# Stick-breaking tails as two rounded passes, 400-column row groups and no engine barriers in a two-block transformer kernel

## The reference, cut to what matters

```
z = (q @ k.T) * scale
log_beta = log_sigmoid(z)
log_keep = where(past, log_sigmoid(-z), 0)
tail = reverse_cumsum(log_keep) - log_keep      # sum over the later keys
a = where(past, exp(log_beta + tail), 0)
out = a @ v
```

## Time and profile before

| | before |
|---|---|
| time, median of 3 runs | 1644.75 us (1641.38 to 1645.51) |
| profiled execution, own time | 1644.14 us |
| its span, first to last instruction | 1642.3 us |
| TensorE busy | 1589.6 us, 97% |
| VectorE, ScalarE, GpSimd busy | 888.2, 669.4, 120.6 us |
| mean granted TensorE clock | 0.996 of full speed |

### The profile page before, as it was taken

One profiled execution on the slowest core, in us unless ns is written; L12 is line 12 of the kernel. 1 busy time (PEld: TensorE's weight loads), 2 busy tenths in 40 slices (PEclk: granted clock), 3 DMA queues, 4 the chain that ended last, 5 costly groups with the idle time before them and its releaser, 6 DMA issues.

```text
span 1642.3 us, 27109 instructions
## 1 busy us (share of the span) xinstructions
PE 1589.6 (97%) x11727; PEld 1285.9 (78%) x11727; DVE 888.2 (54%) x1386; ACT 669.4 (41%) x1005; POOL 120.6 (7%) x138
## 2 busy tenths in 40 slices
PE   7999999998999999999999999999899999999998
PEld 5856778776895798888888898777568888888887
DVE  5455586442634364555454654436875766555644
ACT  4316843324334264334141254656883532221210
POOL 1310106000000010000000020012300000000000
PEclk9999999999999999999999999999999999999999
DMA  7611223320630335536453533321003243333322
GB/s 241 185 52 52 76 89 100 113 85 30 198 132 23 128 123 187 183 105 228 128 179 128 179 87 109 77 77 52 2 27 103 62 118 85 96 103 103 94 78 86
DMA packets 154073, 176.66 MB, mean 108 GB/s; under 512 B 14600, under 2 KB 111506, under 8 KB 153570
## 3 DMA queue, kind: packets, MB, share of 16 engines
q1 hardware_dynamic: 145004, 162.24, 31.0%
q10 hardware_dynamic: 8950, 12.69, 2.6%
HBM read 168.31 MB, written 8.43 MB: 108 GB/s over the span
## 4 chain that ended last, share of the span: by engine, by line
PE 85%; DVE 7%; ACT 5%; issue 2%; DMA 1%; ACTq 0%; SPq 0%; DVEq 0%; POOL 0%
PE ps L397 63%; PE ps L848 4%; PE ps L1471 4%; PE ps L824 1%; PE ps L2066 1%; PE ps L3135 1%; DMA sb_arena<-sb_arena 1%; DVE weights_low L420 1%; PE ps L2892 1%; ACT weights_high L417 1%; PE ps L2880 1%; PE ps L2912 1%; PE ps L1049 1%; PE ps L765 1%; DVE sb_hT L2988 1%
## 5 line engine op out<-in xcount | busy, mean ns | idle before, releaser
L420 DVE TENSOR_TENSOR weights_low<-sb_weights_raw,weights_high 128x2048 fp32r<-128x2048 f32 (+2 forms) x117 | 263.9, 2255 | 260.2 <-ACT weights_high L417 260.0
L397 PE MATMUL ps<-left_high,weights_high 128*128 128x512 f32 (+1 forms) x888 | 352.0, 396 | 2.3 <-DVE left_low L718 2.1
L397 PE MATMUL ps<-left_low,weights_high 128*128 128x512 f32 (+1 forms) x888 | 345.9, 390 | 0.0
L397 PE MATMUL ps<-left_high,weights_low 128*128 128x512 f32 (+1 forms) x888 | 345.9, 390 | 0.0
L417 ACT CAST weights_high<-sb_weights_raw 128x2048 fp32r<-128x2048 f32 (+2 forms) x117 | 219.4, 1875 | 299.3 <-PE ps L397 261.6
L397 PEld LDWEIGHTS ps<-left_high,weights_high 128*128 128x128 f32 (+1 forms) x888 | 166.0, 187 | 47.5 <-issue 9.2
L397 PEld LDWEIGHTS ps<-left_high,weights_low 128*128 128x128 f32 (+1 forms) x888 | 166.0, 187 | 36.0
L397 PEld LDWEIGHTS ps<-left_low,weights_high 128*128 128x128 f32 (+1 forms) x888 | 166.1, 187 | 35.5 <-issue 1.7
L397 PE MATMUL ps<-weights_high,hidden_high 128*128 128x512 f32 x432 | 169.1, 391 | 0.0
L397 PE MATMUL ps<-weights_high,hidden_low 128*128 128x512 f32 x432 | 168.2, 389 | 0.0
L397 PE MATMUL ps<-weights_low,hidden_high 128*128 128x512 f32 x432 | 168.1, 389 | 0.0
(11 more groups left out here) (445 smaller groups left out, 2463.1 us busy)
## 6 DMA issues: line engine op xcount, KB each, us to landing
sb_weights_raw<-in_w_in SPq DMA_DIRECT2D x25, 1024.0 KB, 5.2
sb_yT<-in_ada_w SPq DMA_DIRECT2D x24, 1024.0 KB, 5.3
sb_weights_raw<-in_ffn_w_up SPq DMA_DIRECT2D x44, 512.0 KB, 4.8
sb_weights_raw<-in_mlp_w_up SPq DMA_DIRECT2D x16, 1024.0 KB, 5.8
sb_weights_raw<-in_mlp_w_down SPq DMA_DIRECT2D x16, 1024.0 KB, 7.5
sb_weights_raw<-in_ffn_w_down SPq DMA_DIRECT2D x10, 1024.0 KB, 5.1
sb_weights_raw<-in_xattn_w_kv SPq DMA_DIRECT2D x8, 1024.0 KB, 5.3
sb_weights_raw<-in_w_out SPq DMA_DIRECT2D x6, 1024.0 KB, 5.1
```

Source lines behind the costliest of these rows:

```text
L397: last = nc.tensor.matmul(o, lhsT, rhs, start=b["first"] and i == 0, stop=b["last"] and i == len(pairs) - 1)
L420: nc.vector.tensor_tensor(l[:, 0:n], raw[:, 0:n], h[:, 0:n].bitcast(F32), ALU.subtract).then_inc(w_low, 1)
```

## The change

- Barriers: `stage_end` and its four uses are gone. In their places stand waits for what is needed: the grams wait per PSUM bank for the inversion's reads, the recurrence waits for all kept grams, TensorE waits for all eight banks of the query projection before cross attention. The grams' first dense step (after the third gram) is left out there and so comes at the grams' end.
- Rows: the 256-column and the 144-column row chunks become one of 400 columns, loaded as two chunks of 4 k-tiles each (upper, lower), four pieces each. As two token tiles fit the two banks, the order is: upper for tiles 0 and 1, lower for them, upper again for tiles 2 and 3, lower again for them ("again" chunks are neither loaded nor split a second time). A step is now 12 multiplications of 400 columns.
- Tails: ScalarE rounds the softplus into EX_HIGH (`high`), VectorE subtracts it in place to get the remainder (`low`), ones and triangle are rounded once into ONES_TRI by VectorE, and TensorE multiplies each block twice, by the high and by the low part.
- Order: the numbers of dense steps between the parts change as shown. SP loads the second half of the bias tables after the chunk 0 to 256 instead of after 1024 to 1280, and waits for all four heads' tails before.

```diff
+        ROWS_AT, ROWS_W = 512, 400
+        def stick_and_sparse_rows():
+            columns = (2052, 2308), (2756, 2820), (2884, 2960), (1536, 1540)
+            def blocks(half, tiles):
+                return [by_token(0, ROWS_W, h_rows(t), "dve", dve_copy_to(VB[:, t, ROWS_AT:ROWS_AT + ROWS_W]), nk=4,
+                                 k0=4 * half, first=half == 0, last=half == 1) for t in tiles]
+            upper, lower = (chunk_of([W2K[:, 4 * half:4 * half + 4, x:y] for x, y in columns], blocks(half, (0, 1)))
+                            for half in range(2))
+            return [upper, lower] + [dict(pieces=[], again=ch, nk=4, width=ROWS_W, blocks=blocks(half, (2, 3)))
+                                     for half, ch in enumerate((upper, lower))]
...
-            chunk_of(w2((2052, 2308)), trow(0, 256, 512)),
+            *stick_and_sparse_rows(),
...
-            chunk_of(w2((2756, 2820), (2884, 2960), (1536, 1540)), trow(0, 144, 768)),
...
         def front_pe(pe):
...
-            fill(dense, 4)
+            fill(dense, 2)
...
             def tails(pair, e):
-                pe.wait_ge(st_sp, 2 * pair + e + 1)
+                pe.wait_ge(split_low, pe.count(split_low))
                 for kt in range(NT):
                     for k2 in range(kt, NT):
                         o = AT_KT[kt] + (k2 - kt) * P
-                        last = nc.tensor.matmul(st_sums(e)[:, o:o + W_KT[k2]], cst("tri") if k2 == kt else ones,
-                                                st_part(EX[e], k2), start=k2 == kt, stop=k2 == NT - 1)
+                        for low, part in enumerate((EX_HIGH[:, e, :], EX_LOW[e])):
+                            last = nc.tensor.matmul(st_sums(e)[:, o:o + W_KT[k2]], ONES_TRI[:, int(k2 == kt), :],
+                                                    st_part(part, k2), start=k2 == kt and not low,
+                                                    stop=k2 == NT - 1 and low == 1)
...
             scores(0)
-            fill(dense, 4)
+            fill(dense, 6)
             tails(0, 0)
...
             scores(1)
-            fill(dense, 4)
+            fill(dense, 6)
             tails(1, 0)
             fill(dense, 1)
             tails(1, 1)
-            fill(dense, 2)
+            fill(dense, 1)
             times_v(1)
...
+            def high(pair, e):
+                a.wait_ge(st_sp, 2 * pair + e + 1)
+                nc.scalar.copy(EX_HIGH[:, e, :], EX[e]).then_inc(split_high, 1)
...
             logs(0)
             nc.scalar.preload_act_table_set(EXP_SET)
             fill(dense, 4)
+            high(0, 0)
+            high(0, 1)
+            fill(dense, 2)
             weights(0, 0)
...
             logs(1)
             nc.scalar.preload_act_table_set(EXP_SET)
-            fill(dense, 4)
-            split_weights(a, "act", w_in_2[6]["index"])
+            fill(dense, 2)
+            high(1, 0)
+            high(1, 1)
+            fill(dense, 2)
+            split_weights(a, "act", w_in_2[8]["index"])
             weights(1, 0)
...
+            def low(e):
+                v.wait_ge(split_high, v.count(split_high))
+                nc.vector.tensor_tensor(EX_LOW[e], EX[e], EX_HIGH[:, e, :].bitcast(F32),
+                                        ALU.subtract).then_inc(split_low, 1)
...
+            nc.vector.tensor_copy(ONES_TRI[:, :, :].rearrange("p a b -> p (a b)"),
+                                  consts[:, cst_at["ones"][0]:cst_at["ones"][0] + 2 * P])
             scaled(0, 0)
             scaled(0, 1)
-            fill(dense, 2)
+            fill(dense, 4)
             softplus(0, 0)
             softplus(0, 1)
+            low(0)
+            low(1)
             fill(dense, 2)
             exponents(0, 0)
...
             fill(dense, 1)
             softplus(1, 0)
             softplus(1, 1)
+            low(0)
+            low(1)
             fill(dense, 3)
+            split_weights(v, "dve", w_in_2[8]["index"])
             exponents(1, 0)
-            split_weights(v, "dve", w_in_2[6]["index"])
...
-            stream_weights(sp, STREAM[w_in_2[4]["index"]:w_in_2[7]["index"]])
+            stream_weights(sp, STREAM[w_in_2[7]["index"]:w_in_2[11]["index"]])
+            sp.wait_ge(st_tail, 4)
             load_bias_sp(sp, range(4, 8))
...
             invert_pe(pe, memory)
-            pe.stage_end()
             grams_pe(pe, memory)
-            pe.stage_end()
             scan_pe(pe)
-            pe.stage_end()
             w_out_pe(pe)
             w_q_pe(pe)
-            pe.stage_end()
+            for bank in range(8):
+                pe.wait_ge(*banks_after(w_q)[0][bank])
```

More of the change, by code:

```diff
@@ L139, with __init__ @@
 class Side:
-    def __init__(self, eng, stage_sem):
-        self.eng, self.wait_ge, self.stage_sem = eng, eng.wait_ge, stage_sem
+    def __init__(self, eng):
+        self.eng, self.wait_ge = eng, eng.wait_ge
         self.seen = {}
@@ L153, in skip @@
         self.count(sem, n)
-    def stage_end(self):
-        self.eng.drain().then_inc(self.stage_sem, 1)
-        self.wait_ge(self.stage_sem, self.count(self.stage_sem, 3))
 def build_program(nc, A, out):
@@ L335, in lay_stream @@
                         b["free"] = opener[b["bank"]]["freed"] = frees[b["owner"]]
-                if mod:
+                if ch.get("again"):
+                    ch["parts_slot"], ch["parts"] = ch["again"]["parts_slot"], ch["again"]["parts"]
+                    parts_free[ch["parts_slot"]] = acc
+                elif mod:
                     raw_free[r] = (mod_used, n_of[mod])
@@ L408, in split_weights @@
                 side.split += 1
-                if ch.get("kind"):
+                if ch.get("kind") or ch.get("again"):
                     continue
@@ L1700, in build_program @@
         N_GRAM_BANKS = 6
+        INV_BANK_READ = [(inv_y_kept, 19), (inv_y_kept, 20), (inv_xt_kept, 22), (inv_xt_kept, 24), (inv_xt_kept, 23),
+                         (inv_xt_kept, 21)]
         def grams_pe(pe, dense):
             for n, (u, lhsT, rhs, dst, mask) in enumerate(ALL_GRAMS):
-                if n >= N_GRAM_BANKS:
+                if n < N_GRAM_BANKS:
+                    pe.wait_ge(*INV_BANK_READ[n])
+                else:
                     kept = gram_by_dve if ALL_GRAMS[n - N_GRAM_BANKS][4] else gram_by_act
@@ L1707, in grams_pe @@
                 chunk_products(n % N_GRAM_BANKS, lhsT, rhs, u).then_inc(gram_done, 1)
-                if n % 3 == 2:
+                if n % 3 == 2 and n > 2:
                     fill(dense, 1)
@@ L1832, in out_of_state @@
                 return last
+            pe.wait_ge(gram_by_dve, 4 * NPAIR)
+            pe.wait_ge(gram_by_act, 2 * NPAIR)
             for u in range(NPAIR):
@@ L2696, in norms_act @@
         def norms_act(a, dense):
-            for i, (tiles, SQ, n, kept) in enumerate(((QK[:, 4:8, :], SQ_FOX, 64, 7), (QK[:, 0:4, :], SQ_DIFF, 32, 9))):
+            for i, (tiles, SQ, n, kept) in enumerate(((QK[:, 4:8, :], SQ_FOX, 64, 9), (QK[:, 0:4, :], SQ_DIFF, 32, 11))):
                 columns_kept(a, kept)
@@ L2736, in front_act @@
             dense = evac_steps(a, "act", w_in_2)
-            fill(dense, 12)
+            fill(dense, 10)
             for i in range(2):
@@ L3640, in _ @@
         def _(eng):
-            a = Side(eng, stage_sem)
+            a = Side(eng)
             a.split = 0
@@ L3666, in _ @@
         def _(eng):
-            v = Side(eng, stage_sem)
+            v = Side(eng)
             v.split = 0
```

31 lines of the change are left out of this document (14 added, 17 removed).

## The result

The changed kernel takes 1655.99 us (median of 6 runs, 1652.14 to 1660.73), the kernel before, beside it, 1642.66 (1640.22 to 1645.51). The ratio is 1.0091, 95% interval 1.0077 to 1.0105: slower by 12.6 to 17.2 us. The profiled execution took 1655.1, its span 1653.3.

A forecast was written before the change was run, and what follows sets the result against it. TensorE, busy 97% of the span, was taken to bound the kernel. Barriers -2.2, rows -4.6, tails -6.4, new waits +20.0 and clock +3.4 gave +10.2 on 1644.14: 1654.3 us, own range 1649 to 1661.

The forecast's parts named there:

- central case: Whole kernel: slower, 1654.3 us, own range 1649 to 1661, chance 0.56.
- The long wait: Second pair's fill after the scores: TensorE waits 10.5 us for VectorE's remainder of the chunk 1024 to 1280.
- The 1648: Kernel time in us if that chunk's remainder were ready 17 us after the second scores; 11.2 us was the deciding point.
- Tails and rows: Second block's front: tails 2.8 us per head, -6.4 in all; 400-column row groups of 12 at 2.2 us, -4.6.
- The small waits: New TensorE waits in the front: first pair 1.5, 0.5 and 1.5 us, after the last tails 1.2, before head-norm sums 3.0.
- the wait behind ScalarE's DMA issues: After the stick part, TensorE waits 2.1 us for chunk 768 to 1024, behind ScalarE's DMA issues, rounding and VectorE's remainder.
- costs nothing: SP's new wait for the fourth tails: no cost, as ScalarE needs the chunks some 30 us later; uncovered, up to 12.
- the clock: TensorE's clock falls after the 10.5 and 3.0 us waits, 1.7 us each: +3.4, bounds 0 and 6.8.
- The barriers: Removed barriers at grams, scan and cross attention: TensorE waits shrink, -2.2 us, between 0 and -3.3.
- the chunk's remainder is there in time: Rival: VectorE has chunk 1024 to 1280 ready 11.2 us after the second scores; 12.2 less, 1642.1, no change; chance 0.17.
- All new waits are covered: Rival: no new TensorE waits in the front, only the savings remain; 1630.9 us, faster; chance 0.11.
- Every longer wait lowers the clock: Rival: all five waits of 1.5 us and more pay 1.7 each, three more falls, 5.1; 1659.4 us; chance 0.05.

The follow-up runs named there:

- the kernel with the chunk split ahead: Changed kernel with the splitting of columns 1024 to 1280 moved ahead of the second pair's magnitudes (ScalarE) and scaled scores (VectorE); 1.0042 of the kernel before.
- the kernel with four steps ahead of the tails: Changed kernel with four dense steps, not six, before the second pair's first tails and three, not one, after its second; 1.0033 of the kernel before.
- the reordered kernel: Changed kernel with one chunk split ahead, bias loads later and four more moves clearing VectorE or ScalarE from TensorE's way; 1630.97 us, 0.9943 of the kernel before.

## Why the prediction was right

The forecast, slower at 1654.3, met 1655.99 in its central case, and with the cause it named. That the two times lie only 1.7 us apart is in part luck (below). Step by step:

- **The long wait** (10.5): 10.36, ended by the remainder it named, in the order of steps it followed, with the third and fourth tails queued behind. The kernel with the chunk split ahead shows the cause. One sum beside it is off: with the remainder ready at 17, a wait of 5.8 us would be left, and taking 4.7 us off 1654.3 gives 1649.6. The 1648 takes off the fall of the clock too, though the prediction's own row has a fall at 2.06 us; the 6.76 of the kernel with four steps ahead had one.
- **Tails and rows** (2.8 a head, 2.2 a group of 12): 2.73 and 2.19. Taking 0.111 us for 128 columns was a little dear.
- **The small waits** (1.5, 0.5, 1.5, 1.2, 3.0): 1.29, 0.37, 1.20, 1.07, 2.88, all in their places; 0.9 us less in sum.
- **Mis-sized: the wait behind ScalarE's DMA issues** (2.1): 4.35. The step that failed is the sentence that SyncE's new wait "costs nothing". I asked only who waits for the chunks queued behind the bias loads. I did not ask what those loads do to another engine's issues at that moment: ScalarE's took 4.68 us, and 2.01 with the loads later, where the wait was 1.68.
- **Mis-sized: the clock** (+3.4, two falls at 1.7): three falls. 2.45 behind the long wait (8.19 against 5.74), 2.07 behind the 4.35 (7.82 against 5.75), and 1.52 behind the 2.88 (4.40 for 24 products of 256 columns, at 0.120 us each 2.88): 6.0. The wait of 4.35 was to be 2.1 and to pass without a fall, and the one price, 1.7 for every fall, was too low for two of the three.
- **The barriers** (-2.2): by the times -0.8, between -2.6 and +1.0, which neither refutes nor shows it; by the waits in the trace -2.0. The first two barriers gave 1.3, the third 1.0, the last -0.2, where I had 1.2, 0.95 and 0.05.

So the front came to +17.0 where the terms give -4.6 - 6.4 + 20.0 + 3.4 = +12.4: 2.6 of the miss is the clock, 1.2 the waits; 0.8 is not assigned. Part of it may be that a bracket counts from the modelled end of a record: the product ahead of the wait of 1.29 began at 981.48, 1.64 us before the next, where the pace is 0.18, so 1.46 were lost. By the ratio the change costs 12.6 to 17.2 us, and my sum was 10.2. The time came out closer than the sum by luck: the profiled execution it was added to, 1644.14, stood 1.5 above the later median of the kernel before.

The rivals: "the chunk's remainder is there in time" could be run, as the chunk split ahead. It gave 8.0 and not the 12.2 I had priced, because a wait for a bank (2.38) and its fall of the clock took the place of the first. "All new waits are covered" is nearly the reordered kernel: 9.4 faster than before, where I had 13.2. "Every longer wait lowers the clock" was nearer than its 0.05: of the waits in the front that are shown here, those of 0.37 to 1.29 us were followed by no fall, and those of 1.68, 2.38, 2.88, 4.35, 6.19, 6.76 and 10.36 were. The Trainium skill, "TensorE: Matmul & The Clock Gate", section "HAM oscillation — how this bites in real kernels", has a kernel in which every wait between groups is followed by a cold start; the traces agree for the seven longer waits just named, and not for those of 0.37 to 1.29 us.

## What to carry to other kernels

When a step is made cheaper for the engine that bounds the kernel by giving two steps to its helpers, write down the helpers' queues in order: look for work that the bounding engine needs soon and that stands late in those queues. Here the splitting stood late even without the new steps (6.19 us of waiting), and the new steps ahead of it added 4.2. The same rounded tails were worth 0 in one order and 4.6 us in another, and moving one splitting ahead gave back 8. And when a DMA is put behind a new wait, look also at which other engine issues DMAs at the moment it is let go.

## What was not expected of the hardware

- DMA issues on one engine take longer right behind another engine's loads: two issues on ScalarE took 4.68 us with four loads of 448 KB issued by SyncE from 2.5 us earlier on, and 2.01 without them (4.54 to 5.12 in all six traces with these loads just ahead, 2.00 to 2.40 in the six others). Whether the loads' issue or their transfers do it is not shown.
- The price of a fall of the clock does not follow the length of the wait: 1.52 us behind the 2.88 of the changed kernel and 2.61 behind the 2.87 of the kernel with the chunk split ahead (4.40 and 5.49 for the same 24 products); 1.61 behind 1.68, 2.45 behind 10.36. And behind one wait of 2.06 us, in much the same code, it fell in six of twelve traces and not in the others.
- The clock also falls without a wait of TensorE: in the kernel before to 0.57 from 1124 to 1128, behind 167 us with 0.35 us of idle time, at a price of 1.4 (24 products in 4.47 against 3.06).
